# Two 2048-wide layers on one core: projections in groups of 1024 columns on four PSUM banks, heads between their panels on the other four

## The reference

```python
h = rmsnorm_2(x, attn_norm[l])
proj = h @ w_in[l]                                   # 2048 x 4928
c_q, c_kv, k_rope, rq, rk, rv, rg = split(proj)      # 512, 256, 64, 1024, 1024, 1024, 1024
q  = rmsnorm_2(c_q,  q_norm[l])  @ w_uq[l]           # 512 x 1536, 8 heads of 128 + 64 (rope)
kv = rmsnorm_2(c_kv, kv_norm[l]) @ w_ukv[l]          # 256 x 2048, 8 heads of 128 (k) + 128 (v)
a  = causal softmax attention, 8 heads               # scores, mask, softmax, values
r  = causal retention, 8 heads: rope on rq, rk; (q k^T * decay) v; group norm per head; * silu(rg)
mixed = concat(rmsnorm_2(a, beta_attn[l]), r * beta_ret[l])
x = x + mixed @ w_o[l]                               # 2048 x 2048
h = rmsnorm_2(x, mlp_norm[l])
x = x + square(relu(h @ w_up[l])) @ w_down[l]        # 2048 x 8192, 8192 x 2048
# after both layers: rmsnorm_2(x, final_norm)
```

## Time and profile before

| | |
|---|---|
| median of 3 runs | 3379.35 us (3377.25 to 3379.91) |
| span of the profiled execution | 3380.9 us (the page gives no other time of it) |
| PE busy | 3308.9 us, 98% |
| DVE busy | 1858.1 us, 55% |
| ACT busy | 1446.9 us, 43% |
| POOL busy | 346.5 us, 10% |
| read from memory | 594.86 MB, 177 GB/s |

### The profile page before, as it was taken

One profiled execution on the slowest core, in us unless ns is written; L12 is line 12 of the kernel. 1 busy time (PEld: TensorE's weight loads), 2 busy tenths in 40 slices (PEclk: granted clock), 3 DMA queues, 4 the chain that ended last, 5 costly groups with the idle time before them and its releaser, 6 DMA issues.

```text
span 3380.9 us, 44789 instructions
## 1 busy us (share of the span) xinstructions
PE 3308.9 (98%) x17215; PEld 2821.6 (83%) x17215; DVE 1858.1 (55%) x1921; ACT 1446.9 (43%) x1563; POOL 346.5 (10%) x280
## 2 busy tenths in 40 slices
PE   6999999999999999999999999999999999999998
PEld 6988888888888788778888888888877888888887
DVE  6878565555444544555555544454455555554445
ACT  4334454444444543544344444443354444444343
POOL 5332010000000102610000000000053000000000
PEclk9999999999999999999999999999999999999999
DMA  6444556655555455335655555555542565655553
GB/s 191 143 132 149 199 175 187 188 185 197 188 197 190 170 189 179 125 113 183 191 186 186 188 196 191 194 185 188 184 146 96 192 190 185 195 186 193 191 195 140
DMA packets 204650, 598.37 MB, mean 177 GB/s; under 512 B 16136, under 2 KB 57320, under 8 KB 166648
## 3 DMA queue, kind: packets, MB, share of 16 engines
q1 hardware_dynamic: 203096, 589.06, 52.4%
q0 software_dynamic: 1312, 7.41, 0.6%
q10 hardware_dynamic: 144, 0.52, 0.0%
HBM read 594.86 MB, written 2.10 MB: 177 GB/s over the span
## 4 chain that ended last, share of the span: by engine, by line
PE 90%; DVE 5%; ACT 1%; issue 1%; POOL 1%; DVEq 1%; POOLq 0%; ACTq 0%
PE ps L506 48%; PE ps L580 20%; PE ps L586 11%; PE ps L932 2%; DVE wlo L1758 2%; PE ps L653 1%; PE ps L655 1%; PE ps L654 1%; ACT whi L1163 1%; PE ps L536 1%; PE ps L1088 1%; PE ps L1087 0%; PE ps L1059 0%; PE ps L1118 0%; PE ps L1082 0%
## 5 line engine op out<-in xcount | busy, mean ns | idle before, releaser
L1758 DVE TENSOR_TENSOR wlo<-raw,whi 128x2048 fp32r<-128x2048 f32 (+1 forms) x546 | 1250.5, 2290 | 1286.8 <-ACT whi L1163 1286.4
L1163 ACT CAST whi<-raw 128x2048 fp32r<-128x2048 f32 (+2 forms) x550 | 1031.3, 1875 | 1519.0 <-PE ps L506 977.7
L506 PE MATMUL ps<-whi,stage 128*128 128x512 f32 x3168 | 793.8, 389 | 2.4 <-DVE wlo L1758 1.2
L580 PE MATMUL ps<-xT,whi 128*128 128x512 f32 x3072 | 733.0, 391 | 0.0
L506 PEld LDWEIGHTS ps<-whi,stage 128*128 128x128 f32 x3168 | 594.2, 188 | 127.6 <-DVE wlo L1758 4.4
L580 PEld LDWEIGHTS ps<-xT,whi 128*128 128x128 f32 x3072 | 564.6, 188 | 109.2
L506 PE MATMUL ps<-whi,xT 128*128 128x512 f32 x1856 | 474.6, 385 | 7.7 <-DVE wlo L1758 7.6
L506 PE MATMUL ps<-wlo,stage 128*128 128x512 f32 x1584 | 432.5, 389 | 0.0
L506 PEld LDWEIGHTS ps<-whi,xT 128*128 128x128 f32 x1856 | 343.2, 188 | 79.1 <-DVE wlo L1758 12.1
L586 PEld LDWEIGHTS ps<-xT,wlo 128*128 128x128 f32 x3072 | 393.9, 191 | 15.0
L586 PE MATMUL ps<-xT,wlo 128*128 128x256 f32 x3072 | 398.5, 283 | 0.0
(11 more groups left out here) (418 smaller groups left out, 2097.8 us busy)
## 6 DMA issues: line engine op xcount, KB each, us to landing
raw<-in_mlp_w SPq DMA_DIRECT2D x128, 1024.0 KB, 5.1
raw<-in_w_up SPq DMA_DIRECT2D x128, 1024.0 KB, 5.3
raw<-in_w_down SPq DMA_DIRECT2D x128, 1024.0 KB, 4.8
raw<-in_w_in SPq DMA_DIRECT2D x100, 1024.0 KB, 5.1
raw<-in_w_o SPq DMA_DIRECT2D x32, 1024.0 KB, 4.8
raw<-in_w_out SPq DMA_DIRECT2D x16, 1024.0 KB, 4.9
raw<-in_w_in SPq DMA_DIRECT2D x16, 832.0 KB, 4.5
raw<-in_w_uq SPq DMA_DIRECT2D x8, 768.0 KB, 4.2
```

Of the source, the lines that this page charges most:

```text
L506: last = mm(psum(bank_of(r, n), width), x_of(part, r), w[:, s, at + c0:at + c0 + width], start=start and first, stop=stop and part == 1)
L580: mm(psum(bank + j), whi[:, u % 2, c:c + P], xT[:, k, :], start=k == 0, stop=False)
L1163: act.copy(whi[:, u % 2, 0:width], raw[:, u, 0:width]).then_inc(sig["hi"], 1)
L1758: tt(wlo[:, u % 2, 0:width], raw[:, u, 0:width], whi[:, u % 2, 0:width].bitcast(F32), SUB).then_inc(sig["lo"], 1)
```

## The change

Only the two layers change (the first block's `down` is the old one under the name `down1`).

**Groups.** `w_in`, `w_uq`, `w_ukv` and `w_o` are cut by columns into eleven groups of at most 1024 columns, 64 panels in all: `lat` (the latents and k_rope, 832 columns, 8 panels), `rq` (8), `uq0` (2), `uq1` (2), `kv0` (2), `kv1` (2), `rk`, `rv`, `rg`, `o0`, `o1` (8 each). A panel holds 2 x 128 rows of 1024 columns (1 MB) except in `uq1`, `kv0`, `kv1` (512 KB). A group needs four banks, X or Y: `lat`, `uq0`, `kv0`, `rk`, `rv`, `rg`, `o1` use X, and `rq`, `uq1`, `kv1`, `o0` use Y. While `rk`, `rv`, `rg` fill X, the heads work in Y.

**Panels.** In a panel PE now runs its 16 matmuls with the high part of the weights first, and waits for the low part only ahead of the last 8. The last panel of a group runs bank by bank and waits for its low part at its start.

**Places.** Each panel has three positions, 0, 1 and 2 (after 8, 16 and 24 of its matmuls), and all engines read the same table: softmax head m starts at place 2 + 5m counted from the start of `rk`, retention head h at 45 + 3h. The order of the two kinds is turned round.

**Group norm** moves from POOL to DVE (`bn_stats`, `bn_aggr`, in `ret_moments`, `ret_normalised`). POOL keeps the rotations, now in pieces of 8 heads.

**Sums and transposes.** `o0`/`o1` and the two column halves of `down` let x be summed one half at a time, the first half beside the second half's product; the transposes for the next stage stand between panels. `down` reads `hT` twice, once per half, so its high and low parts (`stage`) are made twice: 128 instructions of 256 columns on ACT and 128 on DVE per layer where there were 64 on each.

```diff
-LAYER = ("pre_attn", "w_in2a", "w_in2b", "w_in2c", "lora_norm", "w_uq", "w_ukv", "rope",
-         "heads", "mixed", "w_o", "add_o", "pre_ffn", "up", "down", "add_ffn")
+LAYER = ("pre_attn", "attn", "lora_norm", "rope", "heads", "mixed", "add_o", "pre_ffn", "up", "down", "add_ffn")
+def mla_turn(m):
+    return 2 + 5 * m
+def ret_turn(h):
+    return 45 + 3 * h
+MLA_SCORES, MLA_PROBS, MLA_VALUES = 2, 5, 7
+RET_SCORES, RET_VALUES = 2, 4
...
+                def product(name, bank, x_of, free, ready=None):
...
+                        pe.wait_ge(sig["hi"], P0 + p + 1)
+                        if end:
+                            pe.wait_ge(sig["lo"], P0 + p + 1)
...
+                        else:
+                            for kk in range(ks):
+                                for r in range(RT):
+                                    for part in range(2):
+                                        for n in range(n_of):
+                                            if begin and kk == part == 0:
+                                                free(r, n)
+                                            one(kk, r, n, part, whi)
+                                    if kk * RT + r == ks * RT // 2 - 1:
+                                        between(p, 0)
+                            between(p, 1)
+                            pe.wait_ge(sig["lo"], P0 + p + 1)
...
+                            last.then_inc(sig["pan"], 1)
+                        between(p, 2)
...
+                def high(p):
+                    act.wait_ge(sig[f"raw{p % 4}"], 16 * (at["quad"] + p // 4 + 1))
+                    act.wait_ge(sig["pan"], P0 + p - 1)
+                    act.copy(whi[:, p % 2, 0:panel_width(p)], raw[:, p % 4, 0:panel_width(p)]).then_inc(sig["hi"], 1)
...
+                def low(p):
+                    dve.wait_ge(sig["hi"], P0 + p + 1)
+                    w = panel_width(p)
+                    tt(wlo[:, p % 2, 0:w], raw[:, p % 4, 0:w], whi[:, p % 2, 0:w].bitcast(F32), SUB).then_inc(sig["lo"], 1)
...
+                def ret_moments(h):
+                    dve.wait_ge(sig["vv"], heads["vv"] + 8 + h + 1)
+                    for r in range(RT):
+                        last = dve.bn_stats(moments[:, 8 * r + h, :], psum(Y + 3, P, at=r * P))
+                    last.then_inc(sig["gn"], 1)
```

More of the change, by code:

```diff
@@ L465, in _ @@
[L465 to L474, removed]
@@ new lines, in columns @@
+                def columns(name, w, c0):
+                    g = GROUP[name]
+                    rows = g["ks"] * P
+                    for i in range(g["n"]):
+                        panel(g["first"] + i, w[i * rows:(i + 1) * rows, c0:c0 + sum(g["widths"])])
+                columns("lat", of("w_in_2"), 0)
+                columns("rq", of("w_in_2"), C_RQ)
+                columns("uq0", of("w_uq_2"), 0)
+                columns("uq1", of("w_uq_2"), 1024)
+                columns("kv0", of("w_ukv_2"), 0)
@@ L478, in _ @@
+                columns("kv1", of("w_ukv_2"), 1024)
+                columns("rk", of("w_in_2"), C_RK)
+                columns("rv", of("w_in_2"), C_RV)
+                columns("rg", of("w_in_2"), C_RG)
+                columns("o0", of("w_o_2"), 0)
+                columns("o1", of("w_o_2"), 1024)
+                up(of("w_up_2"))
+                down(of("w_down_2"))
+                for name in ("pre_attn", "lora_norm", "rope", "heads", "mixed", "add_o", "pre_ffn", "add_ffn"):
                     st.stage(name)
@@ L1035, in _ @@
-                evk, rope = at, st.stage("rope")
-                at = st.stage("heads")
+                X = 4 * layer
+                Y = 4 - X
+                if layer == 0:
+                    pre = norm("pre_attn", dict(resid=sums["resid"]), sums["mo0"])
+                else:
+                    pre = st.stage("pre_attn")
+                at = st.stage("attn")
+                P0 = 4 * at["quad"]
+                lora, rope, heads, mixed = st.stage("lora_norm"), st.stage("rope"), st.stage("heads"), st.stage("mixed")
@@ L1137, in mixer @@
-                def mixer(b):
-                    if b == 0:
-                        pe.wait_ge(sig["ret"], at["ret"] + 1)
-                    if b == 4:
-                        pe.wait_ge(sig["mla"], at["mla"] + 1)
-                tile_banks(at, lambda k, r: qn[:, r, k - 8, 0:DN] if k >= 8 else
-                           proj[:, r, C_RQ + k * P:C_RQ + (k + 1) * P], mixer)
-                rows("w_o", free=tiles_left(at), first=8)
-                at = norm("pre_ffn", st.stage("add_o"))
-                down(up(at))
+                    if i < 7:
+                        pe.wait_ge(sig["evR"], heads["evR"] + i + 2)
@@ L1723, in _ @@
+                more = layer + 1 < DEPTH2
+                down(up({3: last_rows, 4: lambda: square(0, 12288, R_FFN)}, {2: ffn_root}, Y), next_rows if more else None)
                 st.stage("add_ffn")
@@ L2468, in _, with weights @@
[L2468 to L2474 removed]
+                def weights(m):
+                    dve.wait_ge(sig["xp"], heads["xp"] + m + 1)
+                    if m:
+                        dve.wait_ge(sig["vv"], heads["vv"] + m)
+                    copy(probT, psum(Y + 2, 384)).then_inc(sig["pt"], 1)
+                    dve.reciprocal(hl[:, m, 4:4 + RT], hl[:, m, 2:2 + RT])
```

1322 lines of the change are left out of this document (768 added, 554 removed), and 3 rows, old and new, of the table LAYER.

## The result

The changed kernel takes 3345.39 us (median of 4 runs, 3345.23 to 3345.48), beside 3378.3 for the kernel before in the same comparison: ratio 0.9905, 95% interval 0.9894 to 0.9917, so 32.9 us less. Forecast were 3339 us and 40. The span of the profiled execution went from 3380.9 to 3343.4 us, 37.5 less.

The account below looks back on a forecast made before the run. PE, busy 98% of the span, was taken as the bound. Gains 31.2 + 13.6 + 0.4 = 45.2 us, less 5 of new waits, net 40.2: 3380.9 - 40.2 = 3340.7, less 1.55, so 3339 us; range 3331 to 3364.

Parts of the forecast that it names:

- B: Rival at the heads: half of 56 pieces per layer come 0.2 us early and wait; 27 us, 3361 us; chance 0.09.
- C: Rival in `rk`, `rv`, `rg`: a ring of ACT and DVE waits outlasts a panel; 53 us, 3387 us; chance 0.05.
- D: Rival: clock falls in the interleaved heads, costing 55 us, and the 13.6 aren't won; about 3390 us; chance 0.04.
- the wait at `uq0`'s last panel: PE waits there for a low part slowed by POOL's rotation of `rq`; 1.2 us per layer.
- the median of the runs lies 1.55 us below that span: Last step: from the forecast profiled span, 3340.7 us, to the forecast median of the timed runs, 3339 us.
- Term 2: Mainly at the layers' heads: PE's lower clock returns to full speed, all of it taken as won; 13.6 us.
- Term 1: Both layers: PE's 28 waits, 23.1 us, go, with 0.29 us lost beside each; 31.2 us.
- Term 4: New waits of PE beside panels and heads in the layers; 2.5 us per layer, 5 for both.
- the 0.3 for the first softmax head: PE waits there for DVE's copy of `kv1`, behind a low part slowed by POOL; 0.3 us per layer.
- the 0.4 for chance meetings: Heads: PE waits where work meets by chance at group borders; 0.4 us per layer.
- Term 3: Kernel's end: half of x is squared earlier, leaving two squares of 512 on ACT; 0.4 us gained.
- A: Rival: POOL's rotations slow DVE's low parts beside short panels; 18 us for both layers, 3352 us; chance 0.12.

Follow-up runs that it names:

- e5: Changed kernel plus 36 extra 128x128 matmuls per layer in three panels of `lat`, two after every fourth projection matmul: 3360.19 us.
- e6: Changed kernel plus 36 extra 128x128 matmuls per layer in three panels of `lat`, all twelve of a panel at its end: 3361.37 us.
- e9: Kernel before, plus 28 extra 128x128 matmuls per layer where PE waits longest at the heads: 3375.91 us against 3376.77.
- e13: Changed kernel without the rotation of q and k; one POOL operation of a few elements left per rotation: 3343.18 us.
- e11: Changed kernel; last panels of `uq1`, `kv0`, `kv1` run their high part first, last transposes of `o1` stand one position later: 3341.55 us.
- e4: Changed kernel with the low part of each panel of `rk`, `rv`, `rg` made twice on DVE: 3386.61 us.
- e3: Changed kernel with every panel of the layers' groups waiting for its low part ahead of its first matmul: 3356.37 us.
- e12: Changed kernel with the low part of 1024 columns made once more on DVE in each panel of `rk`, `rv`, `rg`: 3358.32 us.
- e7: Changed kernel with a retention head's values 5 positions behind its transposes instead of 4: 3348.78 us.

## Why the prediction was right, and where its numbers were off

**Right:** the 3331 to 3364 held, and the mechanism is the forecast one. Its signs came: PE's waits in the layers at 1.4 us (8 or less forecast), the clock at 1.00, the head rows gone, and none of B, C and D. One sign did not come, the wait at `uq0`'s last panel. The assumption that a switch of matmuls costs nothing stood the test of e5 and e6.

**The step that failed is the last one, "the median of the runs lies 1.55 us below that span".** Runs whose span and time are both listed show a time 1.8 us above the span (3343.6 and 3345.4, 3378.9 and 3380.7). So the profiled execution of the kernel before, span 3380.9, would have been timed at some 3382.7, slower than any of the three runs shown. Its mean clock was 0.993; the runs of that kernel show 0.994 to 0.997, and half of them take 3376 to 3377 us. It was one of the executions that lost most to the clock. The same offset for after gives 3340.7 + 1.8 = 3342.5 instead of 3339.1: 3.4 of the 6.3 us of error; the span's own 2.7 are nearly all of the rest. It also explains why the span fell by 37.5 us and the median by 32.9: the clock's term is real, but is that of one execution.

**Term 2, the clock, 13.6 us.** Summed over the starts of the matmuls in the layers (distance to the next start, less the median distance for the same matmul at full clock), the half clock cost 12.1 us in that execution. It fell three times in the layers, not twice as the prediction has it: twice at the heads of layer 0 and once at those of layer 1, for 30.7 us in all. Windows of the kernel before:

```profile
1426.00:1441.00 15.00, 14.52 (x51) 0.54 0.00 0
1457.00:1465.00 8.00, 6.34 (x29) 0.57 0.00 1
2563.00:2574.00 11.00, 9.43 (x45) 0.53 0.01 1
```

In the median run it cost 5 to 7, by e9. The prediction's remark that idle time alone hardly explains the clock at the heads is answered by e9 as well: with that time filled and all the transposes kept, the clock stayed at 1.00.

**Term 1, the waits, 31.2 us.** The price of 0.29 us beside each wait was read at a 512-column matmul, but 18 of the 28 waits stand ahead of shorter ones (16 of 128 columns, 2 of 256). There it is less. The row behind such a wait in the kernel before:

```profile
1417.09 0.39 PE L1120 MATMUL ps<-big 128*128 128x128 f32 x2
1418.64 0.30 PE L1059 MATMUL ps<-cst,big 128*128 128x128 f32 x1 [1.17 <-DVE small L2388]
1418.78 0.27 PE L1060 MATMUL ps<-cst,under_xT 128*128 128x128 f32 x1
```

The second of the two matmuls of the first row starts at 1417.20; 1.44 - 0.11 = 1.33 us were lost where the row says 1.17, and the next start comes after 0.14 instead of 0.11: 0.19 in all. With this price for all 18, an estimate from one row, 23.1 + 10 x 0.29 + 18 x 0.19 = 29.4.

**Term 4, new waits, 5 us.** Measured 1.4 + 4 x 0.29 = 2.6. The wait at `uq0`'s last panel (1.2 per layer) didn't come: DVE's low part was not stretched at all, POOL's operation was. A row of each in the changed kernel, at the same time, the POOL operations beside it taking 1.3 us:

```profile
1241.95 2.29 DVE L2596 TENSOR_TENSOR wlo<-raw,whi 128x2048 fp32r<-128x2048 f32 x1 [1.25 <-ACT whi L1778]
...
1242.06 3.34 POOL L2984 TENSOR_TENSOR big<-big,rope_cs 128x512 f32<-128x512 f32 x1
```

Wherever the two met in these traces, the one that started later was stretched, by about what was left of the other: here POOL's, which started 0.11 us behind the low part, and at `kv0`'s last panel (e13) DVE's, which started 0.16 us behind a POOL operation. The 3.69 us of the earlier trace rows fit this: the low part began at 1343.37, POOL's operation of the earlier trace rows ended at 1345.32, and 1.95 + 1.89 = 3.84. So the stretch is no factor, but at most the rest of one POOL operation, and these are half as long now (1.3 us beside 2.40). Up to `kv1` a low part took at most 1.35 times its time alone, in `rv` 1.47 (3.37 us). The narrow panels came as forecast (gaps of 0.43 and 0.25 us per layer beside 0.6). Nothing was seen of the 0.3 for the first softmax head and the 0.4 for chance meetings. One wait I had not named: `o1`'s last panel, 0.62 per layer, where the low part stands on DVE behind a transposed tile's, which waits for ACT.

**Term 3, the tail, 0.4 us.** PE's last matmul in the trace starts 11.1 us ahead of the end in the kernel before and 10.9 in the changed one, whose very last matmul (0.2 us later) has no record: about 0.5 us gained. The prediction read six squares in the earlier trace rows; they are three, with three readings of their sums, which changes nothing in the term.

**Sum.** With these sizes, 29.4 + 12.1 + 0.4 - 2.6 = 39.3 us of span, against 37.5 measured. If the new waits are put at what e11 gained by their removal, 3.9 instead of 2.6, it is 38.0; the 0.5 us left are not explained. For the timed runs the clock's 5 to 7 us stand in place of 12.1: 30.9 to 34.2 us, beside 32.9 measured. That the forecast span came within 2.7 us is in part luck: terms 1 and 2 were 3.3 us too large, and term 4, with most of its places wrong, was 1.1 to 2.4 too large the other way.

**The rivals.** A is true in kind and far too dear: priced at 18 us, 2.2 in all (e13). B's 27 us fall with PE's waits. C does not occur; e4 shows that even with 2.3 us more of DVE work per panel the loss sits at single places. (The 1.1 us a panel in C's price is worked out nowhere in the prediction, and D's "about 3390" is 3394 by its terms: 3380.9 - 40.2 + 55 - 1.55.) D falls: with the same transposes and short matmuls between projections the clock is 1.00.

**What the parts gave:** of the 32.9 us, 11 hang on the order within a panel once the heads stand between panels (e3), and the rest comes without it. How much the column halves of `down` and the group norm on DVE gave by themselves was not tried.

## What to carry to other kernels

Move latency-bound chains between pieces of the bound engine's work with two or three pieces of cover at each tie, and give the bound engine first the part of its work that is ready first. Here the move, with the smaller parts of the change, gave some 20 us without that order, the order without the move nothing clear, and both together 33. Before adding up a profile, set its span and its mean clock beside those of the timed runs: a term read from one execution's half clock belongs to that execution. Slack is a matter of places, not of averages: look for the panels that need their whole input at the start, and for the first use behind a stage border.

## What the runs showed of the hardware

- The clock fell to 1.2 GHz behind or within waits of PE of 1.1 to 5 us, and stayed there for 3 to 14 us, mostly with PE busy (e4's windows; in the kernel before the longest lies between 1426 and 1441). Each of e4's waits of 2.0 and 5.0 us and of e12's of 3.2 us had such a fall; single waits of 1.0 to 1.4 us in e3, e4 and e7 had one in one case of ten. The mean clock differs from run to run, 0.994 to 0.997 in the kernel before, and its times scatter by 3 to 7 us where those of the changed one, at 0.998 throughout, scatter by 0.3 to 1.7.
- A plain fp32 128x128 matmul appears as two records of 0.11 us each.
- Coming back from a short piece, the first 512-column matmul starts early and the second late (in the changed kernel at 1325.49, 0.03 us behind the last short one, and the second 0.32 us behind the first instead of 0.227). This costs nothing measurable (e5, e6).
- DVE's low parts and POOL's rotations side by side slow one or the other, in the rows here the one that started later: a POOL operation took 3.34 us instead of 1.3, or a DVE one 1.66 instead of 1.22.
